# First causal layer: values made token by channel behind the index scores, attention started 64 ticks later at 3.5 ticks a step, and one total issued earlier in the second block

## The chip, the cores and the metric

One core of one Trainium2 chip. The metric is the device time of one execution in microseconds; the kernel before takes 2296.45 us (median of 3 runs, 2296.16 to 2297.04).

## What is computed

A transformer in fp32 on 512 tokens of 1024 channels: a first block with two layers (attention, then a convolutional FFN), then a second block with three branches and an FFN. Only the first layer of the first block and the seam between the blocks matter here. Layer 0, cut down:

```python
h = rmsnorm(x, attn_norm[0])
qa, ka, va, qb, kb, vb, qi, ki, wi = split_cols(h @ w_in_even[0], sizes_even)
# a-heads 0..7: attention over blocks of 256 keys; with two blocks this is all of the causal keys
# b-heads 8..15: each query keeps the 128 keys with the highest index score
rel = relu(einsum('bqhd,bsd->bqhs', qi, rmsnorm(ki)) * 64 ** -0.5)
score = einsum('bqhs,bqh->bqs', rel, wi)            # causal, then top-k
x = x + concat([o_a, o_b]) @ w_o[0]                 # o = softmax(q k^T / 8 + bias) @ v
```

At the seam: `x1 = rmsnorm(x, final_norm)`, and the second block begins with `rms_norm(x1, norm_mix) * (1 + m) + s`, so the factor of a token needs the mean square of x and that of its gated norm.

## The kernel before, in words

Activations lie channel by token: `XT`, 8 tiles of 128 channels by 512 tokens. Each GEMM in fp32 is three products of fp32r parts, high by high, low by high and high by low (`pe_steps`, L487 to L489). A weight unit is 128x1024: SP loads it into `raw` (three buffers), ACT writes the high part `wH` (L469), DVE the low part `wL` (L474). Both stay three units ahead. The order of all units is written out in `weight_units`.

**Ticks.** Every engine runs the same order of layer 0, `layer_order`, through `follow`. A tick is one k of a unit, that is three matmuls on PE; a unit has 8 ticks (4 in the output projection `wo0`). ACT, DVE and SP have their share of a unit at fixed ticks of it: DVE writes the low part of a later unit at its middle (fifth tick), and evicts q or k at its last; ACT makes the high part of q or k at the second tick of the next unit, and POOL its low part (`po_lows`, L1588).

**Order of layer 0 before.** Unit `ki`, eight units `qi`, then per head pair p the units q, k, v, then 16 units `wo0`: 328 ticks. The index scores (24 items: four matmuls, a relu on ACT, two weighted additions on DVE) start after tick 58, one every two ticks. At tick 108 the attention starts. It has 34 steps here named s (32 of work, four to a head pair, for query blocks 3, 1, 2, 0 of 128 rows). In its first half PE issues scores (L1437), DVE takes them off with bias and row minimum (L1521) and ACT exponentiates both heads (L1483); in its second half DVE takes reciprocals (L1529), ACT scales (L1504; from s = 16 on DVE scales one head of the two) and PE transposes the step before (L1469), which ACT copies out (L1495). PE's scores of a step wait for DVE's L1521 of the step before, its transposes for the scaled rows, and the transposes of block 3 also for L1521 of the step after. After block 0 come the products with the values (L1454), `mixH` on ACT and `mixL` on DVE (L1511).

**Keep rounds.** The top-k is 16 rounds of `max` and `match_replace` for each of three query blocks (512, 256 and 384 wide) and one selection for each: 51 calls of `ve_keep` on DVE (L1164 to L1169), placed in the order as `("keep", n)` behind the second half of a step. The masked bias of steps from 16 on (POOL, L1607) needs them all.

**Pace before.** Ticks between the halves and behind them: (4,3) for 6 steps, (3,3) for 18, (2,2) for 6, (2,1) for 4; two or three keep calls in each of the first 18 steps.

**Values before.** A v unit gives channel by token; ACT copies the bank to `hf` (L954), PE turns it in four transposes (L858, `turn` in `pe_fill`), and ACT writes `vR` token by channel in four scaled copies (L922). `vR` has three slots.

**Layer 1** makes its values the other way already: `values` in `pe_fill` has `hH`, `hL` slices of 128 tokens as the stationary side and the weights as the moving side (L878 to L880), each unit holding two k of 512 channels, four banks at a time; ACT takes each bank off with one scaled 128x512 copy into `vAll` (L961). Its attention runs 28 steps at 4 ticks a step and 6 at 3, without index scores or keep calls.

**The seam.** `pe_block2` (L2208 on) first runs four context units of eight tiles (`pe_tile`, L2196 to L2198, 256 wide). `pe_end_sums` (L1776) sums the gated squares by a matmul with ones, behind the second of these units. Its result goes through ACT (L2282, L2284: factor `rr`) to DVE's `hf` (L2331), ACT's `hH` and DVE's `hL` (L2324), for which the first 512 wide tiles of the second block wait.

Of the kernel before, what the change touches and what calls it, by code (L numbers as in the profile page):

```python
# [60 lines left out]
def weight_units():  # L61

    out = []

    def block(up, down):
        for half in range(2):
            for j in range(HALF):
                n = half * HALF + j
                out.append((up, n))
                out.append((up, 22 + n))  # L70
            for m in range(8):
                out.append((down, half * 8 + m))
# [24 lines left out]

KTS = {"we": 8, "wq1": 8, "wv1": 8, "win": 8, "wbr": 4, "wout": 8}
# [51 lines left out]
def build_in(nc, t, out, ctx):  # L150
# [82 lines left out]
    vR = sb("vR", [128, 3, 4, 128])  # L233
# [515 lines left out]
    def layer_units(layer):  # L749
        names = [("we", 0, "ki", 0)] + [("we", 1 + c, "qi", c) for c in range(8)] if layer == 0 else []  # L750
        if layer:
            names += [("wv1", n, "V", n) for n in range(8)]
        for p in range(8):
            for i, kind in enumerate("qk" if layer else "qkv"):
                names.append(("we", 9 + (p // 4) * 12 + 4 * i + p % 4, kind, p) if layer == 0 else
                             ("wq1", 8 * i + p, kind, p))
        names += [(f"wo{layer}", 8 * half + m, "wo", m, half) for half in range(2) for m in range(8)]
        return [Unit(layer, u, *x) for u, x in enumerate(names)]
# [34 lines left out]
    def evicted(x):  # L793

        if x.kind == "ki":
            return ev_v.at((x.n, "w"))
        if is_split(x):
            return qk_s.at(x.n)
        if x.kind in ("q", "k", "qi"):
            return ev_v.at(x.n)  # L800
        if x.kind == "v":
            return vt_c.at((x.layer, x.c))
        if x.kind == "V":
            return vt_c.at((1, 0, 2 + x.u % 2))
        if x.kind == "wo":
            return x_s.at(((x.name, x.half), x.c))
        return ev_a.at(x.n)
# [5 lines left out]
    def values_ready(lane, layer, p):  # L813
        lane.wait_ge(*vt_c.at((1, p // 4, 3) if layer else (0, p)))

    def value_rows(layer, p, b):
        return vAll[:, p, b, :] if layer else vR[:, p % 3, b, :]
# [36 lines left out]
    def pe_fill(pe, layer):  # L854
        def turn(x):
            pe.wait_ge(*ev_a.at(x.n))
            for i in range(4):
                ins = pe.do.transpose(x.bank[:, i * 128:i * 128 + 128], hf[x.c % 2][:, i * 128:i * 128 + 128], ident)  # L858
            ins.then_inc(*vt_mm.up((layer, x.c)))

# [5 lines left out]
        def values(x):  # L866

            g, H, L = x.c // 4, *(b[x.n % 3][:, :1024].rearrange("p (k o) -> p k o", k=2) for b in (wHb, wLb))
            pe.wait_ge(*low_at(x.n))
            for kk in range(2):  # L870
                k = 2 * (x.c % 4) + kk
                pe.wait_ge(*hl_v.at(("attn1", k)))
                for t_ in range(4):
                    if k == 0:
                        pe.wait_ge(*((up_s.at((0, 21, "g")) if g == 0 else x_s.at((("dn0", 1), 7)) if t_ < 3 else
                                      vt_c.at((1, 0, 0)))))
                    o, rows = value_bank(g, t_), slice(128 * t_, 128 * t_ + 128)
                    pe.do.matmul(o, hH[:, k, rows], H[:, kk, :], start=k == 0, stop=False)  # L878
                    pe.do.matmul(o, hL[:, k, rows], H[:, kk, :], start=False, stop=False)
                    ins = pe.do.matmul(o, hH[:, k, rows], L[:, kk, :], start=False, stop=k == KD - 1)  # L880
                    if kk and t_ == 3:
                        ins.then_inc(*gemm.up(x.n))
                    elif k == KD - 1:
                        ins.then_inc(*vt_mm.up((1, g, t_)))
                    yield

        for x in fill[layer]:
            if x.kind == "V":
                for i, _ in enumerate(values(x)):
                    if i == 1 and x.u == 1:  # L890
                        pe_total(pe, "attn1", S)
                    if i == 2 and x.u == 2:
                        pe_factor(pe, 1)
# [9 lines left out]
            before_ = fill[layer][x.u - 1] if x.u else x  # L903
            for i, _ in enumerate(pe_steps(pe, x.n, [part], 1)):
                if i == (1 if x.kind == "wo" else 3) and before_.kind == "v":
                    turn(before_)
# [8 lines left out]
    def ac_fill(ac, layer):  # L915
        def turn(x):
            ac.wait_ge(*vt_mm.at((layer, x.c)))
            if x.c >= 3:
                ac.wait_ge(*at_pv.at((attn[layer].key, x.c - 3)))
            ac.wait_ge(*rt_c.at(layer))  # L920
            for b in range(4):
                ins = ac.do.activation(vR[:, x.c % 3, b, :], x.bank[:, b * 128:b * 128 + 128], ACT.Identity,  # L922
                                       scale=rsT[:, b, 0:1])
            ins.then_inc(*vt_c.up((layer, x.c)))

        for x in fill[layer]:
            before_ = fill[layer][x.u - 1] if x.u else x
            for i in range(x.ticks):
# [6 lines left out]
                if i == (1 if x.kind == "wo" else 3) and before_.kind == "v":  # L935
                    turn(before_)
# [11 lines left out]
            elif x.kind == "v":  # L948
                ac.wait_ge(*gemm.at(x.n))
                if x.c >= 2:  # L950
                    ac.wait_ge(*vt_mm.at((layer, x.c - 2)))
                elif x.c == 0 and layer == 0:
                    ac.wait_ge(*ev_v.at((at["we", 0], "w")))
                ac.do.activation(hf[x.c % 2][:], x.bank, ACT.Copy).then_inc(*ev_a.up(x.n))  # L954
            ac_high(ac, x.n + 3)
            if x.kind == "V" and x.c % 4 == 3:
                g = x.c // 4
                ac.wait_ge(*rt_c.at(1))
                for t_ in range(4):
                    ac.wait_ge(*(vt_mm.at((1, g, t_)) if t_ < 3 else gemm.at(x.n)))  # L960
                    ac.do.activation(vAll[:, 4 * g:4 * g + 4, t_, :], value_bank(g, t_).rearrange("p (c d) -> p c d", c=4),  # L961
                                     ACT.Identity, scale=rsT[:, t_, 0:1]).then_inc(*vt_c.up((1, g, t_)))
            if x.kind == "wo" and x.half == 1:
                z = f"ffn{layer}"
                ac.wait_ge(*x_s.at(((x.name, 1), x.c)))
                if x.c == 0:
                    ac_last_total(ac, z)
                    ac.wait_ge(*gemm.at(qkv(layer, "k" if layer else "v", 7).n))
# [4 lines left out]
    def ve_fill(ve, layer):  # L973
        for x in fill[layer]:
# [43 lines left out]
            elif x.kind == "V" and x.u == 2:  # L1018
# [396 lines left out]
    def pe_pairs(pe, a):  # L1415
        for s in range(35):
            if s < 32 and s % 4 < 2:
                p = s // 4
                these = (s, s + 1) if s % 4 == 0 else (s + 1, s + 2)
                if s == 0 and a.layer == 0:  # L1420

                    pe.wait_ge(*sc_rl.at(23))
                elif s == 0:
                    values_ready(pe, 1, 7)
# [21 lines left out]
            if (p := a.end_of(s - 2)) is not None:  # L1446
# [4 lines left out]
                for b in range(4):  # L1451
                    for u in range(2):
                        c0 = 64 * u
                        ins = pe.do.matmul(bank[7][c0:c0 + 64, 128 * b:], value_rows(a.layer, p, b)[:, c0:c0 + 64],  # L1454
# [127 lines left out]
    def po_lows(po, a, p):  # L1582

        for kind in "qk":
# [5 lines left out]
    def po_masked(po, a):  # L1590
# [623 lines left out]
    def pe_block2(pe):  # L2214
        ns = [unit2(*x) for x in front2]
        pe.wait_ge(*up_s.at((1, 21, "g")))
        for i, n in enumerate(ns):
# [5 lines left out]
            if i == 1:  # L2223
                pe_end_sums(pe)
# [1129 lines left out]
def lay(i):  # L3354
# [8 lines left out]
    for l in range(2):  # L3363
# [20 lines left out]
    we = g["w_in_even"][0]  # L3384
    o["we"] = np.concatenate([pack(np.concatenate([we[:, 4096:4176], np.zeros((D, 48), np.float32)], 1)),
                              pack(we[:, 3072:4096]), pack(we[:, :3072])], 0)
# [36 lines left out]
```

## Time and profile before

| what | value |
|---|---|
| median of 3 runs | 2296.45 us |
| the profiled execution | 2296.61 us |
| its span | 2294.8 us, 30499 instructions |
| PE busy | 2281.1 us (99%) |
| DVE busy | 1438.1 us (63%) |
| ACT busy | 1107.9 us (48%) |
| granted TensorE clock | 0.998 |
| layer 0, index scores to the end of attention | about 47 to 282 us |

The span is from the first to the last instruction; 1.8 us of the execution lie outside it. A matmul's busy time has its pipeline in it: a 128x512 one is shown with 0.39 us, but the next starts 0.23 us later. So the distance from start to start is what one costs PE, and a short stall can hide in a matmul that looks longer.

### The profile page before, as it was taken

To read this page: it belongs to the slowest core of one execution; us is meant where nothing else is said; L and a number is where in the kernel's file an instruction comes from. 1 tells how busy PE (TensorE), PEld (TensorE's weight loads), DVE (VectorE), ACT (ScalarE), POOL (GpSimd) and SP (SyncE) were. 2 spreads that over 40 slices of the span, in tenths; PEclk is the share of its full clock that TensorE was granted. 3 is DMA by queue.
4 is the path that set the end of the run, shared out by engine and by line. 5 is a ranking of instruction groups with operands and counts; after the bars stand their busy time and mean duration, and the time that the engine had idled before them with its cause. 6 is when DMAs were issued, how large, how long until landed. Compare 5 with 4: busy or idle time off the path is not lost. (4 is left out here: it accounts for less than half of the span.)

```text
span 2294.8 us, 30499 instructions
## 1 busy us (share of the span) xinstructions
PE 2281.1 (99%) x11966; PEld 1885.7 (82%) x11966; DVE 1438.1 (63%) x2318; ACT 1107.9 (48%) x1801; POOL 396.4 (17%) x297
## 2 busy tenths in 40 slices
PE   9999999999999999999999999999999999999998
PEld 8877788888888778888888878888888889888887
DVE  7898569858644666773676475557778335543543
ACT  6666654324434555442444366775555234432442
POOL 0013222202210001220222130001102122220222
PEclk9999999999999999999999999999999999999999
DMA  5222144433423223443343231011112432332231
GB/s 192 74 83 84 56 165 147 165 102 124 150 84 101 93 60 132 157 168 117 110 152 105 85 106 56 11 49 56 56 51 74 129 109 89 111 101 93 92 113 62
DMA packets 70222, 233.05 MB, mean 102 GB/s; under 512 B 8032, under 2 KB 10208, under 8 KB 69952
## 3 DMA queue, kind: packets, MB, share of 16 engines
q1 hardware_dynamic: 70080, 231.11, 30.3%
q8 instruction: 95, 1.56, 0.3%
q14 instruction: 47, 0.39, 0.1%
HBM read 224.18 MB, written 4.28 MB: 100 GB/s over the span
## 5 line engine op out<-in xcount | busy, mean ns | idle before, releaser
L487 PE MATMUL psum<-hH,wH 128*128 128x512 f32 (+1 forms) x1840 | 732.2, 398 | 0.6 <-DVE hL L641 0.3
L489 PE MATMUL psum<-hH,wL 128*128 128x512 f32 (+1 forms) x1840 | 714.6, 388 | 0.0
L488 PE MATMUL psum<-hL,wH 128*128 128x512 f32 (+1 forms) x1840 | 713.8, 388 | 0.0
L474 DVE TENSOR_TENSOR wL<-raw,wH 128x1024 fp32r<-128x1024 f32 (+2 forms) x353 | 446.3, 1264 | 362.1 <-ACT wH L469 361.0
L469 ACT ACTIVATE wH<-raw 128x1024 fp32r<-128x1024 f32 (+2 forms) x353 | 363.5, 1031 | 503.6 <-PE psum L489 476.7
L489 PEld LDWEIGHTS psum<-hH,wL 128*128 128x128 f32 x1840 | 345.3, 188 | 71.3
L487 PEld LDWEIGHTS psum<-hH,wH 128*128 128x128 f32 x1840 | 345.8, 188 | 70.6 <-issue 4.3
L488 PEld LDWEIGHTS psum<-hL,wH 128*128 128x128 f32 x1840 | 346.2, 188 | 61.3 <-issue 0.7
L2030 POOL TENSOR_TENSOR sg<-sg,cv 128x512 f32<-128x512 f32 x66 | 95.1, 1441 | 677.1 <-ACT sg L1857 677.1
L487 PE MATMUL psum<-gH,wH 128*128 128x512 f32 x506 | 197.0, 389 | 0.0
L489 PE MATMUL psum<-gH,wL 128*128 128x512 f32 x506 | 196.9, 389 | 0.0
L488 PE MATMUL psum<-gL,wH 128*128 128x512 f32 x506 | 196.8, 389 | 0.0
L536 POOL TENSOR_TENSOR ssum<-ssum,sq 128x512 f32<-128x512 f32 (+1 forms) x45 | 66.0, 1467 | 399.0 <-ACT sq L529 393.3
L1634 DVE TENSOR_TENSOR XT<-psum,XT 128x512 f32<-128x512 f32 x64 | 44.1, 689 | 114.0 <-PE psum L489 113.9
L489 PEld LDWEIGHTS psum<-gH,wL 128*128 128x128 f32 x506 | 95.0, 188 | 19.8
L488 PEld LDWEIGHTS psum<-gL,wH 128*128 128x128 f32 x506 | 95.0, 188 | 19.7
L487 PEld LDWEIGHTS psum<-gH,wH 128*128 128x128 f32 x506 | 95.0, 188 | 19.7
L1857 ACT ACTIVATE sg<-cg 128x512 f32<-128x512 f32 x66 | 41.8, 633 | 132.7 <-DVE cg L1955 132.7
L2032 POOL TENSOR_TENSOR gL<-sg,gH 128x512 fp32r<-128x512 f32 x66 | 87.9, 1332 | 49.0 <-ACT gH L1861 49.0
L1483 ACT ACTIVATE Pr<-Sp,mn 128x512 f32<-128x512 f32 (+3 forms) x128 | 70.8, 556 | 49.4 <-DVE mn L1521 49.3
L1861 ACT ACTIVATE gH<-sg 128x512 fp32r<-128x512 f32 x66 | 41.8, 633 | 102.8 <-POOL sg L2030 102.8
L1946 DVE TENSOR_TENSOR hf<-psum,rs 128x512 f32<-128x512 f32 x88 | 60.5, 687 | 42.2 <-PE psum L489 26.3
(402 smaller groups left out, 3532.1 us busy)
## 6 DMA issues: line engine op xcount, KB each, us to landing
raw<-in_up SPq DMA_DIRECT2D x132, 512.0 KB, 3.2
raw<-in_dn SPq DMA_DIRECT2D x48, 704.0 KB, 4.0
raw<-in_win SPq DMA_DIRECT2D x56, 512.0 KB, 3.3
mbuf<-in_wmod SPq DMA_DIRECT2D x48, 512.0 KB, 3.3
raw<-in_we SPq DMA_DIRECT2D x33, 512.0 KB, 3.4
tm<-toep SPq DMA_DIRECT2D x32, 256.0 KB, 4.3
raw<-in_wo SPq DMA_DIRECT2D x32, 256.0 KB, 2.6
raw<-in_wq SPq DMA_DIRECT2D x16, 512.0 KB, 3.3
```

Source lines behind the costliest of these rows:

```text
L469: ac.do.activation(flat_of(wHb, n), flat_of(rawb, n), ACT.Copy).then_inc(*w_hi.up(n))
L474: ve.do.tensor_tensor(flat_of(wLb, n), flat_of(rawb, n), flat_of(wHb, n).bitcast(F), ALU.subtract).then_inc(*w_lo.up(n))
L487: pe.do.matmul(o, H[:, k, :], high(k), start=k == 0, stop=False)
L488: pe.do.matmul(o, H[:, k, :], low(k), start=False, stop=False)
L489: ins = pe.do.matmul(o, L[:, k, :], high(k), start=False, stop=k == kt - 1)
L536: lane.do.tensor_tensor(ssum[:, :n], ssum[:, :n], sq[k % 2][:, :n], ALU.add).then_inc(*own.up((z, k)))
L1483: ac.do.activation(Pr[:, s % 2, u, :W], Sp[:, u, :W], ACT.Exp, scale=-1.0, bias=mn[:, h:h + 1, i], accum_out=den[:, h:h + 1, i]).then_inc( ...
L1634: ve.do.tensor_tensor(xt(m), b, xt(m), ALU.add).then_inc(*x_s.up((key, m)))
L1857: ac.do.activation(sg[q][:], cg_[q][:], ACT.Silu).then_inc(*sg_a.up((layer, n)))
L1946: ve.do.tensor_tensor(of_[:], bank[b], rs[:], ALU.mult).then_inc(*up_s.up((layer, n, what)))
L2030: po.do.tensor_tensor(sg[q][:], sg[q][:], cv[q][:], ALU.mult).then_inc(*sg_p.up((layer, n)))
L2032: po.do.tensor_tensor(gL[:, j, :], sg[q][:], gH[:, j, :].bitcast(F), ALU.subtract).then_inc(*gl_s.up((layer, half, j)))
```

## The change

Layer 0 gets the values of layer 1's kind: eight units `wv0`, packed by the host as `wv1` is, between the second and the third head pair. Units are now `ki`, `qi` x8, q0, k0, q1, k1, V x8, q2, k2 ... q7, k7, `wo0` x16, again 328 ticks. The copies to `hf`, the 32 transposes and `vR` go. The last four index items come a tick apart. 21 keep calls stand behind the scores, one every three ticks, then 7 ticks, and the attention starts at tick 172 with 3.5 ticks a step for 28 steps and 3 for 6, two keep calls in each of the first 15. All of it waits for all values (`values_ready(pe, a.layer, 7)`). POOL's low part of k moves to the start of its own head pair. Apart from that, `pe_end_sums` moves from behind the second context unit to behind the third tile in it.

```diff
     out += [("we", n) for n in range(9)]
-    out += [("we", 9 + (p // 4) * 12 + 4 * i + p % 4) for p in range(8) for i in range(3)]
+    out += [("we", 9 + 2 * p + i) for p in range(2) for i in range(2)]
+    out += [("wv0", n) for n in range(8)]
+    out += [("we", 9 + 2 * p + i) for p in range(2, 8) for i in range(2)]
...
             out_ = [("ticks", 58)]
             for n in range(24):
-                out_ += [("ticks", 1), ("index", n), ("ticks", 1)]
-            out_.append(("ticks", 2))
-            per = [(4, 3)] * 6 + [(3, 3)] * 18 + [(2, 2)] * 6 + [(2, 1)] * 4 + [(0, 0)]
-            last = 2 + 32
+                out_ += [("ticks", 1), ("index", n), ("ticks", 1 if n < 20 else 0)]
+            out_ += [("ticks", 3), ("keep", 1)] * 21 + [("ticks", 7)]
+            per = [(2, 2), (2, 1)] * 14 + [(2, 1)] * 6 + [(0, 0)]
+            last = 8 + 32
         for s, (n, m) in enumerate(per):
-            keep = [("keep", 2 if s < 2 else 3)] if a.layer == 0 and s < 18 else []
+            keep = [("keep", 2)] if a.layer == 0 and s < 15 else []
...
-        def turn(x):
-            pe.wait_ge(*ev_a.at(x.n))
-            for i in range(4):
-                ins = pe.do.transpose(x.bank[:, i * 128:i * 128 + 128], hf[x.c % 2][:, i * 128:i * 128 + 128], ident)
-            ins.then_inc(*vt_mm.up((layer, x.c)))
...
-                    if k == 0:
-                        pe.wait_ge(*((up_s.at((0, 21, "g")) if g == 0 else x_s.at((("dn0", 1), 7)) if t_ < 3 else
-                                      vt_c.at((1, 0, 0)))))
+                    if k == 0 and g and t_ == 3:
+                        pe.wait_ge(*vt_c.at((layer, 0, 0)))
+                    elif k == 0 and layer:
+                        pe.wait_ge(*(x_s.at((("dn0", 1), 7)) if g else up_s.at((0, 21, "g"))))
+                    elif k == 0:
+                        pe.wait_ge(*(sc_rl.at(23) if g or t_ < 2 else evicted(qkv(0, "kq"[t_ - 2], 1))))
...
-            for b in range(4):
-                ins = ac.do.activation(vR[:, x.c % 3, b, :], x.bank[:, b * 128:b * 128 + 128], ACT.Identity,
-                                       scale=rsT[:, b, 0:1])
-            ins.then_inc(*vt_c.up((layer, x.c)))
...
-                if s == 0 and a.layer == 0:
-
-                    pe.wait_ge(*sc_rl.at(23))
-                elif s == 0:
-                    values_ready(pe, 1, 7)
+                if s == 0:
+                    values_ready(pe, a.layer, 7)
...
             if s % 4 == 1 and s // 4 < 7:
-                po_lows(po, a, s // 4 + 1)
+                po_lows(po, a, s // 4 + 1, "q")
+            elif s % 4 == 0 and s > 16:
+                po_lows(po, a, s // 4, "k")
...
             for k in range(KD):
                 pe_tile(pe, n, c_part(pe, bank[2 * i + 1][:, :CTX]), k)
-            if i == 1:
-                pe_end_sums(pe)
+                if (i, k) == (1, 2):
+                    pe_end_sums(pe)
```

## Rows read from the trace of the kernel before

**Rows 1.** The page: busy time, share and instructions of each engine

```profile
PE 2281.1 (99%) x11966; PEld 1885.7 (82%) x11966; DVE 1438.1 (63%) x2318; ACT 1107.9 (48%) x1801; POOL 396.4 (17%) x297
```

**Rows 2.** Windows, the stretch of all keep rounds: PE, PEld, DVE, ACT, POOL busy

```profile
99.00:206.90 107.90, 106.97 (x601) 82.80 (x600) 98.43 (x259) 73.16 (x166) 17.78 (x13) 1.00 0.27 88
```

**Rows 3.** Timeline of PE around the turn of one v unit

```profile
85.79 0.39 PE L489 MATMUL psum<-hH,wL 128*128 128x512 f32 x1
86.02 0.60 PE L858 MATMUL psum<-cn,hf 128*128 128x128 f32 x4
...
86.69 0.39 PE L488 MATMUL psum<-hL,wH 128*128 128x512 f32 x1
```

**Rows 4.** Timeline of DVE and PE in layer 0's sixth step: reciprocal, then transposes

```profile
140.11 0.17 DVE L1529 RECIPROCAL den<-den 128x2 f32<-128x2 f32 x1 [0.36 <-ACT Pr L1483]
...
142.55 0.63 PE L1469 MATMUL psum<-cn,Pr 128*128 128x128 f32 x4 [0.69 <-ACT Pr L1504]
```

**Rows 5.** Timeline of PE, layer 1: block 3 scores of two head pairs, 4 steps apart

```profile
760.33 0.73 PE L1437 MATMUL psum<-kHr,qr 64*128 64x512 f32 x4
...
778.65 0.73 PE L1437 MATMUL psum<-kHr,qr 64*128 64x512 f32 x4
```

**Rows 6.** Lines of DVE in 99 to 206.9: count, busy, mean ns, idle before

```profile
L474 DVE TENSOR_TENSOR wL<-raw,wH 128x1024 fp32r<-128x1024 f32 x13 | 18.7, 1436 | 0.5 <-ACT wH L469 0.5
L1521 DVE CUSTOM_DVE_ANT_0 Sp<-psum,tm 128x256 f32<-128x256 f32 (+3 forms) x30 | 13.0, 470 | 0.0
...
L1529 DVE RECIPROCAL den<-den 128x2 f32<-128x2 f32 x18 | 2.9, 163 | 5.1 <-ACT Pr L1483 5.0
...
L1005 DVE SCALAR_TENSOR_TENSOR qk<-psum,rs 128x512 f32<-128x512 f32 x4 | 2.8, 688 | 0.5 <-PE psum L489 0.5
```

**Rows 7.** Lines by form, DVE in 14 to 290: the maximum of a 512 wide keep round

```profile
L1164 DVE MAX8 m<-sco 128x8 f32<-128x512 f32 x16 | 11.1, 695 | 0.5
```

**Rows 8.** Timeline of DVE: two 256 wide keep rounds, two 384 wide ones

```profile
150.99 0.43 DVE L1164 MAX8 m<-sco 128x8 f32<-128x256 f32 x1
...
151.98 0.43 DVE L1164 MAX8 m<-sco 128x8 f32<-128x256 f32 x1
...
180.51 0.56 DVE L1164 MAX8 m<-sco 128x8 f32<-128x384 f32 x1
...
181.76 0.56 DVE L1164 MAX8 m<-sco 128x8 f32<-128x384 f32 x1
```

**Rows 9.** Timeline of DVE: the reciprocal of a block 3 step with no unit work before it

```profile
124.32 0.17 DVE L1529 RECIPROCAL den<-den 128x2 f32<-128x2 f32 x1 [1.05 <-ACT Pr L1483]
```

**Rows 10.** Timeline: a low part of weights on DVE, alone and beside POOL

```profile
182.90 1.22 DVE L474 TENSOR_TENSOR wL<-raw,wH 128x1024 fp32r<-128x1024 f32 x1
...
148.90 1.99 DVE L474 TENSOR_TENSOR wL<-raw,wH 128x1024 fp32r<-128x1024 f32 x1
...
148.51 1.29 POOL L1588 TENSOR_TENSOR kLr<-qk,kHr 128x512 fp32r<-128x512 f32 x1 [3.21 <-ACT kHr L934]
```

**Rows 11.** Timeline of ACT and DVE: one index item of 384

```profile
92.25 0.81 ACT L1135 ACTIVATE Pr<-psum 128x768 f32<-128x768 f32 x1 [0.27 <-PE psum L1127]
...
91.01 1.27 DVE L1149 SCALAR_TENSOR_TENSOR sco<-Pr,wiR,sco 128x384 f32<-128x384 f32 x2 [0.81 <-ACT Pr L1135]
```

**Rows 12.** Timeline of ACT, layer 1: after the fourth unit of values

```profile
690.95 1.06 ACT L469 ACTIVATE wH<-raw 128x1024 fp32r<-128x1024 f32 x1 [4.38 <-PE psum L880]
691.91 2.41 ACT L961 ACTIVATE vAll<-psum,rsT 128x512 f32<-128x512 f32 x4
```

**Rows 13.** Timeline of DVE and PE at the seam

```profile
1265.42 1.82 DVE L1994 TENSOR_TENSOR hf<-hf,hf 128x512 f32<-128x512 f32 x1
...
1269.45 1.02 PE L1780 MATMUL psum<-hf,cn 128*128 128x512 f32 x2
...
1273.06 0.28 PE L2198 MATMUL psum<-hcH,wL 128*128 128x256 f32 x1
1274.40 0.50 PE L2196 MATMUL psum<-hH,wH 128*128 128x512 f32 x1 [1.06 <-DVE hL L2324]
```

More of the change, by code:

```diff
@@ L95, in weight_units @@
     return out
-KTS = {"we": 8, "wq1": 8, "wv1": 8, "win": 8, "wbr": 4, "wout": 8}
+KTS = {"we": 8, "wq1": 8, "wv0": 8, "wv1": 8, "win": 8, "wbr": 4, "wout": 8}
 for _l in range(3):
@@ L232, in build_in @@
     q_rows = [sb(f"qr{i}", [128, 4 * N_SLOT], R, at=tails[4 * i]) for i in range(2)]
-    vR = sb("vR", [128, 3, 4, 128])
     vAll = sb("vAll", [128, 8, 4, 128], at=mix_at + 16384)
@@ L750, in layer_units @@
         names = [("we", 0, "ki", 0)] + [("we", 1 + c, "qi", c) for c in range(8)] if layer == 0 else []
-        if layer:
-            names += [("wv1", n, "V", n) for n in range(8)]
+        made = [("wv1", n, "V", n) if layer else ("wv0", n, "V", n) for n in range(8)]
         for p in range(8):
-            for i, kind in enumerate("qk" if layer else "qkv"):
-                names.append(("we", 9 + (p // 4) * 12 + 4 * i + p % 4, kind, p) if layer == 0 else
-                             ("wq1", 8 * i + p, kind, p))
+            if p == (0 if layer else 2):
+                names += made
+            for i, kind in enumerate("qk"):
+                names.append(("wq1", 8 * i + p, kind, p) if layer else ("we", 9 + 2 * p + i, kind, p))
         names += [(f"wo{layer}", 8 * half + m, "wo", m, half) for half in range(2) for m in range(8)]
@@ L800, in evicted @@
             return ev_v.at(x.n)
-        if x.kind == "v":
-            return vt_c.at((x.layer, x.c))
         if x.kind == "V":
-            return vt_c.at((1, 0, 2 + x.u % 2))
+            return vt_c.at((x.layer, 0, 2 + x.u % 2))
         if x.kind == "wo":
@@ L813, in values_ready @@
     def values_ready(lane, layer, p):
-        lane.wait_ge(*vt_c.at((1, p // 4, 3) if layer else (0, p)))
-    def value_rows(layer, p, b):
-        return vAll[:, p, b, :] if layer else vR[:, p % 3, b, :]
+        lane.wait_ge(*vt_c.at((layer, p // 4, 3)))
     def layer_order(a):
@@ L871, in values @@
                 k = 2 * (x.c % 4) + kk
-                pe.wait_ge(*hl_v.at(("attn1", k)))
+                pe.wait_ge(*hl_v.at((f"attn{layer}", k)))
                 for t_ in range(4):
-                    if k == 0:
-                        pe.wait_ge(*((up_s.at((0, 21, "g")) if g == 0 else x_s.at((("dn0", 1), 7)) if t_ < 3 else
-                                      vt_c.at((1, 0, 0)))))
+                    if k == 0 and g and t_ == 3:
[4 more added lines that the diff above has]
+                        pe.wait_ge(*(sc_rl.at(23) if g or t_ < 2 else evicted(qkv(0, "kq"[t_ - 2], 1))))
                     o, rows = value_bank(g, t_), slice(128 * t_, 128 * t_ + 128)
@@ L883, in values @@
                     elif k == KD - 1:
-                        ins.then_inc(*vt_mm.up((1, g, t_)))
+                        ins.then_inc(*vt_mm.up((layer, g, t_)))
                     yield
@@ L889, in pe_fill @@
                 for i, _ in enumerate(values(x)):
-                    if i == 1 and x.u == 1:
+                    if i == 1 and layer and x.u == 1:
                         pe_total(pe, "attn1", S)
-                    if i == 2 and x.u == 2:
+                    if i == 2 and layer and x.u == 2:
                         pe_factor(pe, 1)
@@ L902, in pe_fill @@
                 part = late_part(pe, x.bank) if x.kind == "qi" else h_part(pe, f"attn{layer}", x.bank)
-            before_ = fill[layer][x.u - 1] if x.u else x
             for i, _ in enumerate(pe_steps(pe, x.n, [part], 1)):
-                if i == (1 if x.kind == "wo" else 3) and before_.kind == "v":
-                    turn(before_)
                 if i == 5 and x.kind == "qi" and x.c == 1:
@@ L915, in ac_fill @@
     def ac_fill(ac, layer):
[L916 to L920, printed above, removed]
-            for b in range(4):
-                ins = ac.do.activation(vR[:, x.c % 3, b, :], x.bank[:, b * 128:b * 128 + 128], ACT.Identity,
-                                       scale=rsT[:, b, 0:1])
-            ins.then_inc(*vt_c.up((layer, x.c)))
         for x in fill[layer]:
@@ L934, in ac_fill @@
                     ac.do.activation(high, full, ACT.Copy).then_inc(*qk_h.up(before_.n))
-                if i == (1 if x.kind == "wo" else 3) and before_.kind == "v":
-                    turn(before_)
                 if i < x.ticks - 1:
@@ L947, in ac_fill @@
                     ac_index_key(ac)
[L948 to L954, printed above, removed]
             ac_high(ac, x.n + 3)
@@ L957, in ac_fill @@
                 g = x.c // 4
-                ac.wait_ge(*rt_c.at(1))
+                ac.wait_ge(*rt_c.at(layer))
                 for t_ in range(4):
-                    ac.wait_ge(*(vt_mm.at((1, g, t_)) if t_ < 3 else gemm.at(x.n)))
+                    ac.wait_ge(*(vt_mm.at((layer, g, t_)) if t_ < 3 else gemm.at(x.n)))
                     ac.do.activation(vAll[:, 4 * g:4 * g + 4, t_, :], value_bank(g, t_).rearrange("p (c d) -> p c d", c=4),
-                                     ACT.Identity, scale=rsT[:, t_, 0:1]).then_inc(*vt_c.up((1, g, t_)))
+                                     ACT.Identity, scale=rsT[:, t_, 0:1]).then_inc(*vt_c.up((layer, g, t_)))
             if x.kind == "wo" and x.half == 1:
@@ L967, in ac_fill @@
                     ac_last_total(ac, z)
-                    ac.wait_ge(*gemm.at(qkv(layer, "k" if layer else "v", 7).n))
+                    ac.wait_ge(*gemm.at(qkv(layer, "k", 7).n))
                 ac_gain(ac, z, x.c)
@@ L1017, in ve_fill @@
                     ve.do.tensor_tensor(kT[:, x.c % 3, :], x.bank, rs[:], ALU.mult).then_inc(*ev_v.up(x.n))
-            elif x.kind == "V" and x.u == 2:
+            elif x.kind == "V" and layer and x.u == 2:
                 ve_factor(ve, 1)
@@ L1453, in pe_pairs @@
                         c0 = 64 * u
-                        ins = pe.do.matmul(bank[7][c0:c0 + 64, 128 * b:], value_rows(a.layer, p, b)[:, c0:c0 + 64],
+                        ins = pe.do.matmul(bank[7][c0:c0 + 64, 128 * b:], vAll[:, p, b, c0:c0 + 64],
                                            PT[:, u, b, 128 * b:], start=b == 0, stop=b == 3)
@@ L1580, in ve_toeplitz, with po_lows @@
         return bias
-    def po_lows(po, a, p):
-        for kind in "qk":
+    def po_lows(po, a, p, kinds="qk"):
+        for kind in kinds:
             x = qkv(a.layer, kind, p)
@@ L3384, in lay @@
     we = g["w_in_even"][0]
+    heads = np.concatenate([we[:, a:a + 128] for c in range(8) for a in
+                            ((c // 4) * 1536 + 128 * (c % 4), (c // 4) * 1536 + 512 + 128 * (c % 4))], 1)
     o["we"] = np.concatenate([pack(np.concatenate([we[:, 4096:4176], np.zeros((D, 48), np.float32)], 1)),
-                              pack(we[:, 3072:4096]), pack(we[:, :3072])], 0)
+                              pack(we[:, 3072:4096]), pack(heads)], 0)
+    values = np.concatenate([we[:, 1024:1536], we[:, 2560:3072]], 1)
+    o["wv0"] = np.ascontiguousarray(values.reshape(4, 2, 128, 2, 512).transpose(3, 0, 2, 1, 4)).reshape(8, 128, 1024)
     wq = g["w_in_odd"][0]
```

## The prediction

> **What bounds the kernel now.** First the page: PE is busy 99% of the span [rows 1], so only what PE issues, or waits for, can move the time. Then the windows over the stretch in which layer 0 finds its top-k: DVE has work in 98.4 of 107.9 us [rows 2], against 63% over the whole span [rows 1]. Here DVE is nearly as full as PE. Then the timelines, read from start to start. A 128x512 matmul costs PE 0.23 us [rows 3]; a tick is three of them, 0.68 us. In the sixth step DVE's reciprocal comes at 140.11 and PE's transposes of that step at 142.55, after 0.69 us of idle time that ACT's scaling ended [rows 4]. That is the one visible stall of PE in layer 0's attention, and it comes when three 512 wide keep rounds a step have been pushing DVE back. So a second limit lies just under the first: the chain L1521, exponential, reciprocal, scaling, transposes, with DVE's keep rounds in the same queue. The reader should see that PE's 99% hides it.
>
> **What goes.** The GEMM work is the same: 8 units by 24 matmuls of 128x512 either way. The turns go. Without one, the matmul behind L489 at 85.79 would start at 86.02 and the next at 86.25; it starts at 86.69 [rows 3], so a turn costs 0.44 us, and eight cost 3.5. The stall of 0.69 us goes with the pace that made it [rows 4]; the first 0.16 of a wait hides in the 0.39 that a matmul is shown with, so it is -0.9 in all. ACT's copies (hf, vR) were not on the path and count nothing. SP loads as many bytes in as many units, in the new order, so its queue is not touched; the cover is the three units that the loads are ahead.
>
> **The seam.** L1780 runs at 1269.45, though its last input is there at 1267.24 (1265.42 and 1.82) [rows 13]. Five tiles sit between the new place and the old, three matmuls of 0.12 us each, so it runs 1.8 us earlier, at 1267.66, and is not late. All behind it is one chain to L2324, for which PE waits: from 1273.06, where 0.12 us would do, to 1274.40 is 1.2 us lost at the first tile [rows 13]; the second and third tile wait again, since DVE and ACT need more for one than PE. I take 1.7 of the 1.8; the ends are 0 (another input late) and 1.8.
>
> **The start of the values.** The first banks wait for the last relu, and the third for DVE's eviction of k1, which stands behind the last index items. These come a tick apart: PE needs 0.68 for the tick and about 0.7 for the item (four matmuls of three quarters of 0.23), DVE 1.27 for an item and one low part of 1.22 among them [rows 10, 11]. From the end of item 20's matmuls: relu 0.8, four items 5.1, the low part 1.2, the causal addition and the eviction 0.3 and 0.69 [rows 6], so 8.1 us. PE wants the bank at about 6.5. +1.7; ends 0.5 (the low part falls elsewhere) and 3.
>
> **The start of the attention.** It waits for the last values: behind V's end ACT first makes a high part and then four copies, done 3.4 us after it started [rows 12]; PE has four ticks, 2.7 us, to fill, and sees the signals a little late. +1.0; ends 0.5 and 2.
>
> **The first 15 steps.** PE: layer 1 takes 18.32 us for four steps with 16 ticks [rows 5]; less 10.9 for the ticks, the attention's own share is 7.4. With 14 ticks, four steps take 16.9 us, 4.2 a step (before: 6.0 and more). From the second half of step 0 to that of step 14, PE needs 59.3.
>
> DVE in the same stretch: 28 keep calls, of which 12 rounds of 256 at 0.99 and 15 of 384 at 1.25 [rows 8], with one selection 30.9 us; L1521 twice a step, 0.87, 14 times 12.2; reciprocals 2.2; six evictions of q and k at 0.69, 4.1; three mixL at the same price, 2.1 [rows 6]; six low parts at 1.22, 7.3 [rows 10]. Sum 58.8, as long as PE's own work, before any wait. But DVE waits between L1521 and the reciprocal for two exponentials: 1.05 where nothing fills it [rows 9], 0.36 behind an eviction [rows 4], nothing behind a low part. With two ticks there I count seven of 14 steps without fill, four with an eviction, three with a low part: 8.8 us. Before, at three or four ticks, it was 5.1 in 18 steps [rows 6]. So DVE's round is 67.6 us against 59.3: 8.3 too long. PE absorbs some: transposes come 2.44 behind the reciprocal when they are late [rows 4], which leaves 1.8 of a 4.2 step, more in the steps with value products. Laying both orders beside each other step by step, DVE crosses PE's limit around steps 10 and 14, and PE waits 5.5 us in all. I take +5.5; ends 0 (the idle times are filled otherwise) and 10 (collisions, below).
>
> **The rest.** Between scores and attention, 63 ticks are 43 us; DVE has 17 calls of 512 at about 1.55 (1.25 times 0.695 over 0.56) [rows 7, 8], four narrow ones, eight low parts: 40 us, covered, and seven ticks without keep calls let it catch up. Were it not, the first steps would start late. Steps 15 on have no keep rounds: DVE needs under 3 of 4.2 us. POOL was busy for 17.8 of 107.9 us [rows 2] and has room; the moved k split has some 6 ticks between its unit's end and its use. Layer 0's end has eight spare ticks instead of two. All 0, ends -0.3 and 2.
>
> **Sum:** -3.5 -0.9 -1.7 +1.7 +1.0 +5.5 = +2.1 us. The profiled execution took 2296.61, 0.16 above the median; I set it against the median: 2298.5.
>
> **Rival 1: the cover holds (0.32).** DVE's idle time before reciprocals shrinks as soon as it is late, or the uneven steps of PE give more slack than I gave, and the stage costs nothing: -3.4, 2293.0. If the values' start is hidden too: -5.1 to -6.1, 2290.3 to 2291.3. For it: before, DVE was as full in 107.9 us and PE lost 0.9 [rows 2, 4]. Against it: there the step was 6 us and more, and ACT's part of the chain does not shrink with the step.
>
> **Rival 2: DVE and POOL collide (0.26, slower).** A low part that took 1.22 alone took 1.99 beside POOL's split of k, which ran from 148.51 to 149.80 [rows 10]. In the first 15 steps POOL makes up to six splits, then its first masks. If each holds up DVE once, 6 x 0.77 = 4.6 us more go through the chain that already decides, and PE waits 10: +6.7, 2303.2. It decides as soon as DVE is behind at all; with DVE in time it costs nothing. For it: L474's mean in the stretch was 1.44 [rows 6]. Against: five low parts before 140 us met none.
>
> The Trainium skill (SBUF — State Buffer, section "SBUF: two separate sides") says that DVE with two SBUF inputs and GpSimd share one port pair as an exclusive lock, the later one blocking fully. By that rule the trace agrees: the low part was late by what was left of the split, 0.8 to 0.9 us, and every such meeting costs a whole remainder and not a share. It says nothing on how often they meet, so it gives this rival a price and no certainty.
>
> **Rival 3: the change does not reach PE.** That values come from another form of matmul at the same 0.23 us is seen in layer 1; were they dearer by 0.01 each, 192 would cost 1.9. I count this in the range.
>
> **Numbers.** A measurement of this kernel can tell about 0.2%, 4.6 us, from no change: 2291.9 and 2301.0 are the bounds. Main case 0.42, itself from 2295 to 2302; rival 1 0.32, of which about half lies under 2291.9, since the seam and the turns are surer than the costs; rival 2 0.26, most of it above 2301.0. Faster 0.2, same 0.52, slower 0.28. The range from 2290.3, rival 1's end, to 2304.5, a little above rival 2.
>
> **What would show it.** Right: no L858 row; waits of PE's L1469 for ACT's L1504 summing to 4 to 7 us in steps 8 to 15, and DVE over 93% busy there; one wait of about 1.5 us on the first values for L1008 and one of about 1 on the first L1437 for L961; L2196's wait for L2324 down from 1.5 us to under 0.5, with L1780 near 1.8 earlier. Wrong: PE without idle time through the first 15 steps (rival 1), or L474 near 1.8 us each there (rival 2), or waits on POOL's L1607, which I priced at nothing.

## The result, and the profile after

| kernel | median us | runs | ratio to before, 95% interval |
|---|---|---|---|
| before | 2296.3 | 6 | |
| changed | 2306.31 (2306.23 to 2308.04) | 6 | 1.0046 [1.0036, 1.0056] |

The changed kernel is 10.0 us slower (0.44%). The prediction, 2298.5 in a range up to 2304.5, was wrong: the time lies above the range, and a change within 0.2% had been called the likeliest.

The page shows PE at 99% again, as before [rows 1]; nothing in its first line gives the loss away.

```profile
PE 2279.2 (99%) x11934; PEld 1883.0 (82%) x11934; DVE 1437.9 (62%) x2318; ACT 1101.0 (48%) x1769; POOL 393.8 (17%) x297
```

PE has 32 instructions less and 1.9 us less busy time, and yet its span is 9.9 us longer (2304.7 against 2294.8). So the loss is idle time of PE, and the view for it is the waits, here those of PE in the changed kernel. Each row has the line that waited, what released it, the us in total, how many times, and the longest.

```profile
PE psum L1405 <- issue: 6.9, 7, 2.0
PE psum L1437 <- ACT Pr L1472: 2.9, 5, 1.0
PE psum L871 <- DVE qk L979: 1.5, 1, 1.5
...
PE psum L1422 <- ACT PT L1463: 1.2, 1, 1.2
...
PE psum L1405 <- ACT vAll L932: 0.8, 1, 0.8
...
PE psum L2166 <- DVE hL L2294: 0.5, 1, 0.5
```

Lines have new numbers: L1405 are the attention scores (L1437 before), L1437 the transposes (L1469), L1422 the products with values, L871 the new values, L1472 ACT's scaling, L1489 DVE's take-off of the scores, L2166 the tiles at the seam. Three of these rows were in the prediction, with their prices: the first values, the first scores, the seam. The other three belong to the attention steps and hold 11.0 us. The prediction had the one of L1437 for ACT's scaling; the greatest is a wait that it did not have at all: scores that wait "for issue" (the profile names no releaser), seven times, always at the head of a head pair.

What they waited for can be read from three engines side by side. Timeline of PE, of DVE and of ACT in the changed kernel, around the head of the second pair (start us, us, engine, line):

```profile
153.29 0.84 PE L1437 MATMUL psum<-cn,Pr 128*128 128x128 f32 x6
...
156.86 0.73 PE L1405 MATMUL psum<-kHr,qr 64*128 64x512 f32 x4 [2.03 <-issue]
```

```profile
153.59 0.41 DVE L1137 MATCH_REPLACE8 sco<-m,sco 128x256 f32<-128x256 f32 x1
153.91 0.28 DVE L1489 CUSTOM_DVE_ANT_0 Sp<-psum,tm 128x128 f32<-128x128 f32 x1
...
157.86 0.69 DVE L1489 CUSTOM_DVE_ANT_0 Sp<-psum,tm 128x512 f32<-128x512 f32 x1 [0.50 <-PE psum L1405]
```

```profile
154.24 0.41 ACT L1451 ACTIVATE Pr<-Sp,mn 128x128 f32<-128x128 f32 x1 [1.05 <-DVE mn L1489]
...
155.03 1.04 ACT L470 ACTIVATE wH<-raw 128x1024 fp32r<-128x1024 f32 x1
155.98 0.79 ACT L1463 ACTIVATE PT<-psum 128x768 f32<-128x768 f32 x1
```

Read from the end: PE's scores at 156.86 follow ACT's copy of the block 2 step, which ends at 156.77. That copy has had its input since PE's transposes ended at about 154.1. But in ACT's queue it stands behind the two exponentials of the block 0 step and a high part of weights; the exponentials wait for DVE's L1489 of block 0, and this one stands behind DVE's keep rounds. PE's scores for a new pair need that copy (`at_c(s - 2)`), because the block 1 scores use a bank that the block 2 transposes were in. And then DVE waits 0.50 us for PE's scores: the chain is a ring. The other six heads agree: each time the scores start 0.09 or 0.10 us after that copy ends (216.37 and 216.47, for one). How ACT came to be late differs. Ahead of the exponentials of block 0 it waited 1.05 us for DVE here, 1.34 before the head at 176.50 and 0.31 before the one at 216.47, but not at all before the one at 195.51, where its queue ran without a pause from 189.51 on.

### The profile page after: what moved, and what is told of

It is laid out like the page before. It is cut to its first block and busy times, and to the rows that moved or that the text cites. A ratio compares the mean times of both kernels' runs of the same rounds, so it can differ in the third digit from the quotient of the medians.

```text
span 2304.7 us, 30402 instructions
## 1 busy us (share of the span) xinstructions
PE 2279.2 (99%) x11934; PEld 1883.0 (82%) x11934; DVE 1437.9 (62%) x2318; ACT 1101.0 (48%) x1769; POOL 393.8 (17%) x297
## 5 line engine op out<-in xcount | busy, mean ns | idle before, releaser
L488 PE MATMUL psum<-hH,wH 128*128 128x512 f32 (+1 forms) x1776 | 707.1, 398 | 0.6 <-DVE hL L642 0.4
L490 PE MATMUL psum<-hH,wL 128*128 128x512 f32 (+1 forms) x1776 | 689.9, 388 | 0.0
L489 PE MATMUL psum<-hL,wH 128*128 128x512 f32 (+1 forms) x1776 | 689.2, 388 | 0.0
L490 PEld LDWEIGHTS psum<-hH,wL 128*128 128x128 f32 x1776 | 333.6, 188 | 68.9
L488 PEld LDWEIGHTS psum<-hH,wH 128*128 128x128 f32 x1776 | 334.0, 188 | 68.1 <-issue 4.6
L489 PEld LDWEIGHTS psum<-hL,wH 128*128 128x128 f32 x1776 | 334.4, 188 | 58.7 <-issue 0.7
```

What stands on the lines that cost most here:

```text
L488: pe.do.matmul(o, H[:, k, :], high(k), start=k == 0, stop=False)
L489: pe.do.matmul(o, H[:, k, :], low(k), start=False, stop=False)
L490: ins = pe.do.matmul(o, L[:, k, :], high(k), start=False, stop=k == kt - 1)
```

## The experiments

Theory A: the ring just read, pushed back by DVE's keep rounds. Theory B: ACT itself is the bound. Theory C: DVE and POOL collide. Times are medians, and "faster" and "slower" are against the changed kernel's 2306.31 unless another is named; the kernel before was at 2295.9 to 2296.0 us beside all of them (single runs 2295.6 to 2297.8).

**Keep rounds left out.** The 32 rounds of the two narrower query blocks are not made, so their top-k is missing.

```diff
-            for r_ in range(KEEP // 8):
+            rounds = KEEP // 8 if i == 3 else 0
+            for r_ in range(rounds):
```

> The changed kernel with the 32 keep rounds of the 256 and 384 wide query blocks left out (so the top-k of these rows is not made); everything else and its order stay. Theory A (DVE's keep rounds push L1489 of the block 0 step back, ACT's exponentials wait for it, and the copy of the block 2 step that stands behind them in ACT's queue holds PE's next scores): the waits of PE in steps 2 to 15, 11.4 us in the changed kernel, fall to about 1, and the time to 2295 us (2293.5 to 2297). Theory B (ACT is the bound, since it scales both heads in these steps and has work for 53 of 74 us): ACT's work is untouched, so at least 7 of the 11.4 us stay, 2302 or more. Theory C (DVE and POOL collide at the port): the collisions stay but DVE has room for them, as A.

2297.41 us, 1.0006 [0.9996, 1.0015]. A window of that kernel over the first steps (its length; then PE, PEld, DVE, ACT and POOL busy; then the granted clock, DMA share, GB/s), its waits of PE, and two instructions of ACT ahead of the head at 208.30:

```profile
141.00:215.00 74.00, 71.33 (x427) 53.42 (x426) 37.59 (x109) 58.96 (x140) 16.78 (x12) 1.00 0.25 79
```

```profile
PE psum L1407 <- issue: 3.1, 7, 0.9
...
PE psum L1439 <- ACT Pr L1474: 1.1, 3, 0.5
```

```profile
205.17 1.05 ACT L470 ACTIVATE wH<-raw 128x1024 fp32r<-128x1024 f32 x1
...
207.41 0.79 ACT L1465 ACTIVATE PT<-psum 128x768 f32<-128x768 f32 x1
```

8.9 of the 10 us go, while ACT's busy time in the stretch rises: B falls as the main cause. But it is 0.4 above the range for A: even with DVE half empty, 4.2 us of idle time stay in the attention, at the same places. Theory B has its share there. Ahead of the head at 208.30 ACT worked without a pause from 202.48 to the end of the copy at 208.20, and PE waited 0.89 us for it; ahead of 154.72 and 190.44 it is the same. At 3.5 ticks a step ACT's queue alone makes PE wait, without any keep round.

**Scaling from ACT to DVE.**

```diff
-        return () if a.layer else (0, 1) if s < 16 else (1,)
+        return () if a.layer else (1,)
```

> The changed kernel with one head of two scaled by DVE from step 0 on, not from step 16 (about 0.5 us a step from ACT to DVE in 16 steps). Theory A: DVE's round gets longer by 0.5 us and the reciprocal's row waits no less, so PE waits 3 to 7 us more: 2309 to 2313 us. Theory B (ACT is the bound): 8 us of work leave ACT, and the time falls by 3 us or more, to 2303 or less.

2313.92 us, 1.0076 [1.0059, 1.0093]: 7.6 us more, just over A's range, and B is out as the main cause: with less work on ACT the kernel is slower. PE's waits rise from 11.0 to 14.6 us, as A said. The lower clock comes on top. The window over the same stretch:

```profile
141.00:215.00 74.00, 65.34 (x357) 49.37 (x354) 60.17 (x178) 42.65 (x98) 10.28 (x8) 0.91 0.20 65
```

ACT is busy 10.7 us less than in the changed kernel (53.35), in part because the kernel gets less far in the same time: PE gets through 357 instructions where it had 386. The granted clock is 0.91: this is taken up at the end.

**The wait moved.** Only the block 1 scores need the bank.

```diff
-                if s and s % 4 == 0:
-
-                    pe.wait_ge(*at_c.at((a.key, s - 2)))
...
                 for q in these:
+                    if s and s % 4 == 0 and q > s:
+                        pe.wait_ge(*at_c.at((a.key, s - 2)))
                     i = a.block_of(q)
```

> The changed kernel with PE's wait for ACT's copy of the block 2 step moved from ahead of the scores of a head pair to behind its block 3 scores (which use other banks; only the block 1 scores need it). Theory A with that wait as the link: block 3 scores (0.77 us) go out while ACT still copies, in seven head pairs, three of them in the late stretch with 1.4 to 2.0 us each; 2 to 5 us faster, 2301 to 2304. Theory A without that link (PE waits for DVE's L1489 or for ACT's scaling instead), or B, or C: within 1 us of 2306.3.

2302.64 us, 1.0027 [1.0016, 1.0038]: 3.7 us faster by one wait moved behind a matmul group. This shows that the wait is a link. The waits of PE in that kernel now name their releasers:

```profile
PE psum L1436 <- ACT Pr L1471: 2.3, 4, 1.0
PE psum L1421 <- ACT PT L1462: 1.9, 2, 1.2
PE psum L1404 <- ACT PT L1462: 1.9, 3, 1.1
...
PE psum L1404 <- DVE mn L1488: 0.7, 1, 0.7
```

"Issue" is gone and the rest is the late chain itself: scaled rows, copies and row minima, each a little late.

**Four ticks where the keep rounds are, three elsewhere.**

```diff
-            per = [(2, 2), (2, 1)] * 14 + [(2, 1)] * 6 + [(0, 0)]
-            last = 8 + 32
+            per = [(2, 2)] * 16 + [(2, 1)] * 18 + [(0, 0)]
+            last = 6 + 32
```

> The changed kernel at 4 ticks a step (2,2) for the first 16 steps, which hold all keep rounds, and 3 (2,1) for the other 18; the same 328 ticks but two, which come off the end. Theory A: PE has 0.34 us more work a step to lay over DVE's round in the first 15 steps, 5 us in all, and steps 16 to 27 lose nothing, since DVE has under 3 us of work in 3.9: 2301.5 us (2300 to 2304). Against it: POOL's masks may become late at 3 ticks a step, which would show as waits of L1489 for L1577 and keep the time at 2304 or more.

2299.22 us, 1.0014 [1.0005, 1.0024]: 7.1 us faster, 0.8 below the range. Its greatest stall has moved to the first steps at three ticks, and there theory C has a part. Timelines of POOL, DVE and PE:

```profile
227.13 1.39 POOL L1556 TENSOR_TENSOR qr<-qk,qr 128x512 fp32r<-128x512 f32 x1
```

```profile
227.31 2.29 DVE L475 TENSOR_TENSOR wL<-raw,wH 128x1024 fp32r<-128x1024 f32 x1
229.53 0.28 DVE L1489 CUSTOM_DVE_ANT_0 Sp<-psum,tm 128x128 f32<-128x128 f32 x1
```

```profile
231.52 0.82 PE L1405 MATMUL psum<-kHr,qr 64*128 64x512 f32 x4 [2.41 <-issue]
```

A low part of 1.22 [rows 10] takes 2.29 beside POOL's split, L1489 of the block 0 step comes a microsecond late, and PE's scores wait 2.41. The collision is one part of that stall; the ring passes it on.

**Pace and wait together.** Edit: both of the above.

> The kernel with 4 ticks in the steps that have keep rounds and 3 in the rest (2299.2 us), with PE's wait for the block 2 copy moved behind the block 3 scores as well. Theory A with that wait as the link: PE's waits at the head of pairs, 5.6 us there, shrink by up to 0.77 each, 2296.7 us (2295.5 to 2298). If these waits were DVE's L1489 of the block 0 step itself, no change, 2299.

2295.45 us, 0.9998 [0.9988, 1.0007]: 3.8 us below the pace alone, a little more than expected. The waits of PE in the attention steps:

```profile
PE psum L1404 <- ACT PT L1462: 1.0, 3, 0.4
PE psum L1404 <- DVE mn L1488: 1.0, 1, 1.0
...
PE psum L1436 <- DVE Pr L1503: 0.3, 1, 0.3
```

2.3 us where the changed kernel has 11.0: two edits to the order take most of the attention's loss away, with the same keep rounds.

**Three ticks between the halves.**

```diff
-            per = [(2, 2), (2, 1)] * 14 + [(2, 1)] * 6 + [(0, 0)]
-            last = 8 + 32
+            per = [(3, 1)] * 16 + [(2, 1)] * 18 + [(0, 0)]
+            last = 6 + 32
```

> The kernel with 4 ticks in the first 16 steps and 3 in the rest (2299.2 us), but three ticks between the halves and one behind them in the first 16 steps, not two and two. Theory A has DVE idle between L1489 and the reciprocal where no unit work falls there (7.7 us in the stretch with two and two): three ticks fill more of it, 1 to 3 us faster, 2297 to 2298. If that idle time costs nothing, because DVE makes it up elsewhere, the same 2299.

2301.04 us, 1.0019 [1.001, 1.0029]: not faster but 1.8 us slower than two and two, so the expectation failed. How much slower is not sharp, since both kernels scatter: the fastest runs are 2299.42 and 2298.40. DVE's idle time before reciprocals did not shrink; in 141 to 215 us:

```profile
DVE den L1497 <- ACT Pr L1451: 8.8, 11, 1.6
```

It was 7.7 with two and two. PE's scores at the heads wait 7.2 us in all (5.6 with two and two). Why a third tick between the halves does not help I did not find out; that unit work on ACT then stands ahead of the block 2 copy is a guess.

**The gains by themselves.** On the kernel before, the 32 transposes left out (values in the wrong layout), and apart from that the seam alone.

```diff
-                if i == (1 if x.kind == "wo" else 3) and before_.kind == "v":
-                    turn(before_)
...
-            ac.wait_ge(*vt_mm.at((layer, x.c)))
...
-                if x.c >= 2:
-                    ac.wait_ge(*vt_mm.at((layer, x.c - 2)))
-                elif x.c == 0 and layer == 0:
+                if x.c == 0 and layer == 0:
```

> The kernel before with its 32 transposes of values left out (ACT scales the bank as it is, so the values of layer 0 are channel by token where token by channel is due). It prices what the change takes away from PE by itself. By the rows of before: eight turns at 0.44 us, 3.5 us faster, 2292.5 us; if the turns hid in something, nothing.

2294.24 us, 0.9991 [0.9982, 1.0]: 1.8 us, half of what was expected. Its waits of PE in layer 0:

```profile
PE psum L487 <- ACT vR L919: 0.8, 1, 0.8
PE psum L1464 <- DVE mn L1516: 0.8, 1, 0.8
PE psum L1464 <- ACT Pr L1499: 0.7, 1, 0.7
```

Before, the third was there with its 0.69 [rows 4], the first with 0.2 and the second not at all. So 3.5 us of PE's work went and 1.4 us of new idle time came, to which a part hidden in the matmuls adds: DVE (0.8) and ACT's copies of values (0.6) were so near that nearly half of PE's gain was lost to them.

```diff
-            if i == 1:
-                pe_end_sums(pe)
+                if (i, k) == (1, 2):
+                    pe_end_sums(pe)
```

> The kernel before with only the total of the gated norm moved to behind the third tile of the second context unit. By the rows of before 1.7 us faster (0 to 1.8), 2294.3 us.

2294.22 us, 0.9992 [0.9982, 1.0001]: 1.8 us, as priced. Its wait at the seam is 0.5 where it was 1.5, as in the changed kernel, and a fall of the clock that the profiled execution of before has there is gone (last section).

**The two waits at the start of values and attention.** On top of pace and moved wait, other banks.

```diff
-        return bank[(0, 1, 2, 3, 4, 5, 6, 0)[4 * g + t]]
+        return bank[((4, 5, 6, 3, 0, 1, 2, 4) if layer == 0 else (0, 1, 2, 3, 4, 5, 6, 0))[4 * g + t]]
...
-                        pe.wait_ge(*(sc_rl.at(23) if g or t_ < 2 else evicted(qkv(0, "kq"[t_ - 2], 1))))
+                        pe.wait_ge(*(evicted(qkv(0, "kq"[g == 0], 1)) if t_ == 2 + (g == 0) else sc_rl.at(23 if g else 21 if t_ < 2 else 22)))
...
+            if layer == 0 and x.u == 22:
+                pe.wait_ge(*vt_c.at((0, 1, 2)))
...
-                    values_ready(pe, a.layer, 7)
+                    pe.wait_ge(*vt_c.at((a.layer, 1, 3 if a.layer else 1)))
...
+                if q == 0:
+                    values_ready(pe, a.layer, 7)
```

> The kernel with 4 and 3 ticks and the wait moved (2295.5 us), with other banks for the values of layer 0: the first four tiles in 4, 5, 6, 3 and the next in 0, 1, 2, 4, so that no early tile waits for k1's eviction, and the attention's first scores wait for two copies of four. By the changed kernel's rows PE waits 1.5 us (1.7 from start to start) on the first values and 0.8 (1.0) at the first scores; both should go, 2.5 us faster, 2293 us. If DVE is late behind the index scores anyway, the wait comes back on a later bank or at step 1, and less than 1 us is won.

2292.63 us, 0.9986 [0.9977, 0.9995]: 2.8 us below the kernel without it, as expected, and 3.3 below before. Windows from the first values to step 15: PE has no idle time in the first stretch and 0.7 us in the second.

```profile
93.00:141.00 48.00, 48.00 (x219) 39.27 (x218) 39.02 (x77) 15.22 (x21) 1.29 (x1) 1.00 0.28 92
141.00:215.00 74.00, 73.30 (x432) 55.14 (x432) 63.37 (x192) 58.53 (x136) 14.45 (x12) 1.00 0.24 77
```

This is the fastest version tried. The second stretch in the changed kernel reads:

```profile
141.00:215.00 74.00, 65.61 (x386) 48.87 (x382) 60.90 (x182) 53.35 (x124) 10.36 (x8) 1.00 0.22 72
```

**More keep calls ahead of the attention.**

```diff
-            out_ += [("ticks", 3), ("keep", 1)] * 21 + [("ticks", 7)]
+            out_ += [("ticks", 3), ("keep", 1)] * 17 + [("ticks", 2), ("keep", 1)] * 9 + [("ticks", 1)]
...
-            per = [(2, 2), (2, 1)] * 14 + [(2, 1)] * 6 + [(0, 0)]
+            per = [(2, 2)] * 14 + [(2, 1)] * 20 + [(0, 0)]
...
-            keep = [("keep", 2)] if a.layer == 0 and s < 15 else []
+            keep = [("keep", 2)] if a.layer == 0 and s < 13 else []
```

> The same with 26 keep calls ahead of the attention and not 21 (DVE is busy for 36.6 of 48 us there), and so 13 steps with two of them and not 15, 4 ticks in 14 steps. Theory A (every round taken out of the steps shortens the stretch in which DVE's round is longer than PE's): 0.5 to 2 us less than with 21, about 2292 us. If DVE is late at the first steps for it, the same or more.

2294.99 us, 0.9996 [0.9987, 1.0006]: 2.4 us slower than with 21 calls, so this expectation failed too. The waits of PE:

```profile
PE psum L1406 <- ACT PT L1466: 2.0, 3, 0.9
PE psum L1440 <- ACT Pr L1475: 1.2, 2, 0.9
PE psum L1440 <- DVE Pr L1507: 0.9, 1, 0.9
```

The first two had been 1.0 and nothing, and some of the new ones stand in late steps that hold no keep round, where there are now two more at three ticks. Whether the loss is these, or where unit work falls in the steps, is open: the edit changed both.

## Why the prediction was wrong, step by step

- **What bounds: right in the main.** DVE's keep rounds as the second limit just under PE's 99% is what the run without them shows (8.9 of 10 us), and shifting work from ACT to DVE made it worse. ACT's own queue is a third limit right behind, and the prediction had none for it. Of its own signs, DVE over 93% busy in these steps did not come: it was busy for 60.90 of 74 us, 82%.
- **The first 15 steps: the step that failed.** It said +5.5 with ends 0 and 10. PE lost about 11.

  The size: layer 1 of the same kernel takes 70.8 us for its first four head pairs (738.76 to 809.53), which hold 64 ticks. Layer 0 has 56 ticks there; eight less at 0.68 leave 65.3 us, and it took 76.4 (140.04 to 216.47). Between these two heads the waits of PE hold 5.8 (scores) + 2.6 (transposes) + 1.2 (products) = 9.6 us of idle time, and each hides up to 0.16 us more in the matmul ahead of it.

  The mechanism: DVE's round was not mis-sized much: the reciprocals' waits were 7.6 us against 8.8 said. What was missing is a wait: the prediction gave PE's late work one cause, scaled rows for its transposes, and laid both orders beside each other with that one alone. The scores at the head of a pair also wait for ACT's block 2 copy, and in ACT's queue that stands behind the exponentials of the step after. A DVE row late by 1 us thus reached PE by a second, shorter way, with only 3.5 ticks of cover where it had six; what stands ahead in the queue was asked for DVE and not for ACT. Moving the wait alone gave 3.7 us.

  The kernel before showed it already. The prediction took 2.44 us from reciprocal to late transposes [rows 4] as a fixed length, but in 1.06 of that, between the reciprocal's end at 140.28 and ACT's scaling at 141.34, ACT's timeline of before has the rest of a high part and a copy:

```profile
139.91 1.04 ACT L469 ACTIVATE wH<-raw 128x1024 fp32r<-128x1024 f32 x1
140.86 0.58 ACT L1495 ACTIVATE PT<-psum 128x512 f32<-128x512 f32 x1
141.34 1.11 ACT L1504 ACTIVATE Pr<-Pr,den 128x384 f32<-128x384 f32 x2
```

- **The rest: priced at nothing, cost.** Behind the head at 216.47 there are three more of these waits, 1.1 us, and one of L1437, 0.3: 1.4 us idle in all, about 1.6 from start to start. The run without rounds has the same 1.1 and 0.3 there, so the pace itself does this. The fall of the clock behind 217 us (last section) was priced at nothing as well.
- **The turns: 3.5 as PE's work, 1.8 as time** at the old pace. The 0.9 of the old stall did not return at its place.
- **The seam: right,** 1.8 for 1.7 by the medians. The profiled executions differ by more there, 2.6 us, of which about 0.8 is the fall of the clock in that of before.
- **The start of the values and of the attention: right.** 1.7 and 1.0 were said. The idle times are 1.5 and 0.8, to which comes up to 0.16 hidden; ACT's copies end at 139.99 and the scores start at 140.04. In the timeline of the changed kernel:

```profile
93.30 0.68 DVE L979 TENSOR_TENSOR qk<-psum,rs 128x512 f32<-128x512 f32 x1
...
94.04 0.50 PE L871 MATMUL psum<-wH,hH 128*128 128x512 f32 x1 [1.50 <-DVE qk L979]
...
137.59 2.40 ACT L932 ACTIVATE vAll<-psum,rsT 128x512 f32<-128x512 f32 x4
...
140.04 0.74 PE L1405 MATMUL psum<-kHr,qr 64*128 64x512 f32 x4 [0.80 <-ACT vAll L932]
```

- **Rival 2, the collisions:** it ended on the right side, 2303.2, but by luck and not by its own mechanism. Seven low parts in the stretch took 1.37 us in the mean, so collisions added 7 x 0.15, about 1 us, and not 4.6.

```profile
L475 DVE TENSOR_TENSOR wL<-raw,wH 128x1024 fp32r<-128x1024 f32 x7 | 9.6, 1373 | 0.0
```

  By the Trainium skill (SBUF — State Buffer, section "SBUF: two separate sides") the later of the two engines blocks fully. The trace agrees again, roughly, at the 2.29 us low part above: 1.21 us of POOL's split were left when it started, and it took 1.07 longer than alone. Again the rule does not say how often they meet.
- **Rival 1, the cover holds:** for the change as made it did not. With the pace and the wait mended it nearly does, at 2295.45 us (2.3 us of waits are left), and 2292.63 with the banks.

The sum as measured: -1.8 (seam), -3.5 -0.9 (turns, old stall), +1.7 +1.0 (starts), +11.1 (first steps), about +1.6 (late steps), up to +1.7 for the clock in layer 0 and about -0.8 for the clock at the seam: +10.1, for 9.9 between the profiled executions (12.6 later through layer 0, 2.6 back at the seam).

## What to carry to other kernels

When a change shortens the step of an interleaved pipeline, list every semaphore that the bounding engine waits for and follow each back through the queue of the engine that raises it: the instruction that stands ahead of it there, and not the one that feeds it, may set the time. A second engine at 91% busy in the stretch is a warning that every microsecond taken from the first may come back as a wait. Put the slower pace where the extra work is and the faster where it is not, and place each wait directly ahead of the instruction that needs it.

## What was not expected of the hardware

The granted clock fell in the middle of the kernel, after stalls. Windows of 2 us, four of the changed kernel and then two of the kernel before at the seam (the clock stands behind the five busy times):

```profile
213.00:215.00 2.00, 1.54 (x9) 1.09 (x9) 1.42 (x7) 1.69 (x6) 0.00 (x0) 1.00 0.00 0
215.00:217.00 2.00, 0.53 (x4) 0.54 (x6) 0.17 (x1) 1.95 (x6) 1.25 (x1) 1.00 0.01 4
217.00:219.00 2.00, 2.00 (x13) 1.57 (x10) 1.44 (x5) 0.70 (x2) 0.62 (x2) 0.60 0.00 0
219.00:221.00 2.00, 2.00 (x8) 1.51 (x7) 1.97 (x3) 0.82 (x4) 1.83 (x2) 0.55 0.00 0
```

```profile
1276.00:1278.00 2.00, 2.00 (x5) 1.20 (x6) 1.96 (x4) 0.72 (x1) 0.00 (x0) 0.50 0.00 0
1278.00:1280.00 2.00, 2.00 (x8) 1.57 (x7) 1.96 (x4) 1.20 (x2) 0.00 (x0) 0.65 0.00 0
```

In the changed kernel PE was idle for 0.61 us ahead of its transposes at 213.11 and for 1.82 ahead of the scores at 216.47; then it was granted 0.60 and 0.55, the level of 1.2 GHz with some time at 2.4. Two 128x512 matmuls there start 0.43 us apart, where 0.23 is the rule:

```profile
218.52 0.63 PE L489 MATMUL psum<-hL,wH 128*128 128x512 f32 x1
218.95 0.63 PE L490 MATMUL psum<-hH,wL 128*128 128x512 f32 x1
```

Over the 4 us this is 2 x 0.40 + 2 x 0.45 = 1.7 us of PE's full speed lost, on top of the stalls. That is an upper bound for the time: PE's own work is slower then, but the other engines catch up behind it. The seam of the kernel before shows it. Its two windows lose 2 x 0.50 + 2 x 0.35 = 1.7 us in the same way, after waits of 1.06 and 0.48 us. The kernel without turns has the same code there, and in its profiled execution the clock stayed at 1.00; it waited 2.0 us there instead of 1.5 and gained only 0.8 us on the kernel before over the seam.

With DVE scaling as well, the clock over all of 141 to 215 us was 0.91, which is 6.7 us of 74 at most. With the 3.6 us that PE's waits grew this is more than the 7.6 by which that kernel was slower, so the two overlap, and how they share the 7.6 is not shown. Nor does each stall bring the clock down: the longest of the changed kernel, 2.03 us ahead of 156.86, did not (1.00 over 141 to 215 us). So a stall of a microsecond or two in this kernel can cost up to nearly twice its length, and the versions without long stalls (the wait and the pace together, and the banks) have no such dip in layer 0's attention.
